# The last expert and the tail of a one-core diffusion step: half of the earlier experts' sum added by an identity product, the last chunk turned at unit 2, the last three units by column halves

## The reference

```
for e in range(8):                       # N_EXPERTS
    g, u = split(h @ w_gu_e[e])          # 1024 -> 2 x 2816
    out += gates[:, e] * ((silu(g) * u) @ w_down_e[e])
x = x + g2 * out                         # g2: a row per condition
y = x * rsqrt(mean(x * x) + 1e-6) * final_norm_g
```

## Time and profile before

| | us |
|---|---|
| time, median of 3 runs (lowest, highest) | 1475.29 (1468.94, 1476.71) |
| time of the profiled execution | 1475.58 |
| its span, first to last instruction | 1473.7 |
| PE busy in the span | 1402.7 (95%) |
| DVE busy | 1123.2 (76%) |
| ACT busy | 817.0 (55%) |
| mean granted TensorE clock | 0.970 |

### The profile page before, as it was taken

One profiled execution on the slowest core, in us unless ns is written; L12 is line 12 of the kernel. 1 busy time (PEld: TensorE's weight loads), 2 busy tenths in 40 slices (PEclk: granted clock), 3 DMA queues, 4 the chain that ended last, 5 costly groups with the idle time before them and its releaser, 6 DMA issues.

```text
span 1473.7 us, 17234 instructions
## 1 busy us (share of the span) xinstructions
PE 1402.7 (95%) x6831; PEld 1157.8 (79%) x6831; DVE 1123.2 (76%) x1026; ACT 817.0 (55%) x811; POOL 227.5 (15%) x333
## 2 busy tenths in 40 slices
PE   5899989999999999989999999999999999999994
PEld 1687557799999986777888888988889888898873
DVE  0798665547777555556899899988989989889994
ACT  2532663523223223355677777776777777777761
POOL 3000480000000023010899100000000000000000
PEclk8999999999999999979999999999999999999996
DMA  9857343945454536527799999999999999999971
GB/s 343 305 200 255 124 143 122 314 149 161 154 176 152 188 139 202 188 91 284 252 389 389 357 412 348 379 379 352 409 363 360 389 334 412 368 360 389 368 275 44
DMA packets 115255, 406.06 MB, mean 276 GB/s; under 512 B 7937, under 2 KB 30642, under 8 KB 97762
## 3 DMA queue, kind: packets, MB, share of 16 engines
q1 hardware_dynamic: 108176, 382.24, 69.8%
q0 software_dynamic: 5920, 19.44, 4.4%
q10 hardware_dynamic: 1074, 3.23, 0.6%
HBM read 394.92 MB, written 9.96 MB: 275 GB/s over the span
## 4 chain that ended last, share of the span: by engine, by line
PE 90%; DVE 5%; DMA 2%; ACT 1%; issue 1%; POOL 0%; DVEq 0%; SPq 0%; POOLq 0%; ACTq 0%
PE ps L1633 26%; PE ps L1635 26%; PE ps L1634 26%; DMA raw<-in_ada_w 2%; PE ps L1978 1%; PE ps L1647 1%; DVE ring_lo L1448 1%; PE ps L1767 1%; PE ps L1788 1%; PE ps L1687 1%; PE ps L1889 1%; PE ps L1708 1%; PE ps L1832 1%; DMA xg<-rows_dram,pick_to 1%; PE ps L1934 0%
## 5 line engine op out<-in xcount | busy, mean ns | idle before, releaser
L1448 DVE TENSOR_TENSOR ring_lo<-raw,ring_hi 128x2048 fp32r<-128x2048 f32 (+1 forms) x210 | 452.1, 2168 | 59.8 <-ACT ring_hi L949 58.0
L949 ACT ACTIVATE ring_hi<-raw 128x2048 fp32r<-128x2048 f32 (+1 forms) x210 | 381.9, 1821 | 139.7 <-PE ps L1635 138.4
L1633 PE MATMUL ps<-ring_hi,xe 128*128 128x512 f32 (+1 forms) x576 | 219.3, 381 | 2.3 <-issue 1.6
L1635 PE MATMUL ps<-ring_lo,xe 128*128 128x512 f32 (+1 forms) x576 | 217.0, 377 | 0.0
L1634 PE MATMUL ps<-ring_hi,xe 128*128 128x512 f32 (+1 forms) x576 | 216.8, 376 | 0.0
L1089 DVE TENSOR_TENSOR ring_lo<-raw,ring_hi 128x2048 fp32r<-128x2048 f32 x53 | 120.4, 2288 | 104.1 <-ACT ring_hi L756 103.9
L756 ACT ACTIVATE ring_hi<-raw 128x2048 fp32r<-128x2048 f32 x53 | 101.1, 1913 | 173.4 <-PE ps L1635 157.4
L1448 DVE TENSOR_TENSOR ring_lo_more<-raw,ring_hi_more 128x2048 fp32r<-128x2048 f32 (+1 forms) x70 | 151.8, 2168 | 20.2 <-ACT ring_hi_more L949 19.9
L949 ACT ACTIVATE ring_hi_more<-raw 128x2048 fp32r<-128x2048 f32 (+1 forms) x70 | 127.4, 1820 | 42.2 <-PE ps L1635 42.2
L1633 PEld LDWEIGHTS ps<-ring_hi,xe 128*128 128x128 f32 x576 | 108.9, 189 | 19.9 <-issue 1.8
L1635 PEld LDWEIGHTS ps<-ring_lo,xe 128*128 128x128 f32 x576 | 108.5, 188 | 17.9
(11 more groups left out here) (299 smaller groups left out, 2424.4 us busy)
## 6 DMA issues: line engine op xcount, KB each, us to landing
raw<-in_w_gu_e SPq DMA_DIRECT2D x128, 1024.0 KB, 7.7
raw<-in_w_down_e SPq DMA_DIRECT2D x88, 1024.0 KB, 8.8
raw<-in_ada_w SPq DMA_DIRECT2D x48, 1024.0 KB, 5.4
raw<-in_w_gu_e SPq DMA_DIRECT2D x64, 768.0 KB, 6.1
raw<-in_w_gu SPq DMA_DIRECT2D x44, 512.0 KB, 4.9
raw<-in_w_qkv SPq DMA_DIRECT2D x12, 1024.0 KB, 11.6
raw<-in_w_down SPq DMA_DIRECT2D x11, 1024.0 KB
raw<-in_w_o SPq DMA_DIRECT2D x4, 1024.0 KB, 6.0
```

What stands on the lines that cost most here:

```text
L949: act.activation(ehi[m % RINGM][:, 0:w], raw[:, (MOE_U0 + m) % RAW, 0:w], ACT.Copy).then_inc(hi_ready, 1)
L1448: dve.tensor_tensor(elo[m % RINGM][:, 0:w], raw[:, (MOE_U0 + m) % RAW, 0:w], ehi[m % RINGM][:, 0:w].bitcast(F32), ALU.subtract).then_inc(l ...
L1633: pe.matmul(out, l_hi, r_hi, start=first, stop=False)
L1635: return pe.matmul(out, l_hi, r_lo, start=False, stop=last)
```

## The change

Five edits. (1) The six folds leave g0 to g5. The left halves of the three tiles (columns 0 to 511) are folded on DVE after the last `lo`. The right halves are not folded: PE adds `acc` into the PSUM bank by a product with the identity matrix, in F32, before the last expert's rows are added to the same bank, and one multiplication by g2 serves both. (2) The last chunk is turned before d2 and split at d2 (TURN_LAST_N), into a buffer of its own (`last_hi`, `last_lo`: the place of `xe` for the other parity of experts). (3) PE does e0, e1, e2 for columns 0 to 511 (bank 4) and then again for columns 512 to 1023 (bank 5), and the left half is brought back between e1 and e2 of the right half. (4) y is scaled by its gate while it is split, slot by slot, in two halves; the six pieces have a PSUM bank each, so that PE does not wait for DVE. (5) The squares are summed by halves, DVE reads `meta` before its first addition, and POOL's pairs of dependent instructions are chained by one shared semaphore (the cut diff leaves that last edit and the lists of semaphores out).

```diff
+TURN_LAST_N = 2
+LAST_UNITS = 3
+        last_ssq = sb("last_ssq", [P, TILES, 2])       # declared after ssq
+        last_hi, last_lo = xe[:, (LAST + 1) % 2, 0], xe[:, (LAST + 1) % 2, 1]
+        COMB_BANKS = ((6, 7, 0), (1, 2, 3))
...
# ScalarE: high_eh
-                if NC * e + c:
+                last = (e, c) == (LAST, NC - 1)
+                if NC * e + c and not last:
                     act.wait_ge(unit_used, used_by("down", *((e, c - 1) if c else (e - 1, NC - 1))))
-                    act.activation(eh_hi[:, 4 * half:4 * half + n, :],
+                    act.activation((last_hi if last else eh_hi)[:, 4 * half:4 * half + n, :],
# keep_y, for the last expert
-                    act.activation(y_hi[:].rearrange("p (a n) -> p a n", a=2), ps[:, 4:6, :],
-                                   ACT.Copy).then_inc(ey_hi_ready, 1)
+                    for half in range(2):
+                        act.wait_ge(y_half, half + 1)
+                        act.activation(y_hi[:, half * HALF:(half + 1) * HALF], ps[:, 4 + half, :], ACT.Copy,
+                                       scale=slot_gate[:, e:e + 1]).then_inc(ey_hi_ready, 1)
# in the loop over units (the same on VectorE with low_eh)
-                if kind == "down" and n == 0 and (e, c) == (LAST, NC - 1):
-                    high_eh(e, c)
+                if kind == "down" and n == TURN_LAST_N and (e, c) == (LAST, NC - 2):
+                    high_eh(e, NC - 1)
...
# VectorE, in the loop over units
-                if kind == "gu" and (e, c) == (LAST, NC - 1) and n < 6:
-                    if n == 0:
-                        dve.wait_ge(acc_loaded, 16)
-                        dve.wait_ge(gbc_sb, 16)
-                    fold(n)
# VectorE, after it
+            def low_y(half):
+                cols = slice(half * HALF, (half + 1) * HALF)
+                dve.wait_ge(ey_hi_ready, half + 1)
+                dve.scalar_tensor_tensor(y_lo[:, cols], ps[:, 4 + half, :], slot_gate[:, LAST:LAST + 1],
+                                         y_hi[:, cols].bitcast(F32), ALU.mult, ALU.subtract).then_inc(ey_lo_ready, 1)
+            def add_last(half, k):
+                n, cols = TILES * half + k, slice(half * HALF, (half + 1) * HALF)
+                if half == 0:
+                    dve.wait_ge(x_folded, k + 1)
                 dve.wait_ge(comb_ps, n + 1)
+                dve.tensor_tensor(acc[:, k, cols], ps[:, COMB_BANKS[half][k], :], gbc[:, COND[k], cols],
+                                  ALU.mult).then_inc(x_scaled, 1)
+                dve.wait_ge(x_scaled, n + 1)
+                dve.tensor_tensor(x[:, k, cols], x[:, k, cols], acc[:, k, cols], ALU.add).then_inc(comb_sb, 1)
+            fold(0)
+            fold(1)
+            low_y(0)
+            fold(2)
             dve.wait_ge(meta_ready, 1)
             blocks = dve.value_load(meta[0:1, EXTRA:EXTRA + 1], min_val=0, max_val=EXTRA)
+            add_last(0, 0)
+            add_last(0, 1)
+            low_y(1)
+            add_last(0, 2)
+            for k in range(TILES):
+                add_last(1, k)
...
# TensorE
+            def bring_back(half):
+                if half:
+                    pe.wait_ge(acc_loaded, 16)
+                    for k in range(TILES):
+                        pe.matmul(ps[:, COMB_BANKS[half][k], :], ident[:], acc[:, k, HALF:], start=True, stop=False)
+                pe.wait_ge(ey_lo_ready, half + 1)
+                for k in range(TILES):
+                    for r, part in enumerate((y_hi, y_lo)):
+                        ins = pe.matmul(ps[:, COMB_BANKS[half][k], :], selT[:, k * P:(k + 1) * P],
+                                        part[:, half * HALF:(half + 1) * HALF], start=(r == 0 and half == 0), stop=(r == 1))
+                    ins.then_inc(comb_ps, 1)
-            for m in range(NM):
+            for m in range(NM - LAST_UNITS):
+                    if n == TURN_LAST_N and (e, c) == (LAST, NC - 2):
+                        pe.wait_ge(eh_ready, NC * e + c + 2)
+                        turn_hidden(e, c + 1)
...
+            pe.wait_ge(eh_lo_ready, 2 * NC * N_EXP)
+            for half in range(2):
+                for n in range(LAST_UNITS):
+                    m = NM - LAST_UNITS + n
+                    pe.wait_ge(lo_ready, MOE0 + m + 1)
+                    for r in range(2):
+                        w = slice(r * D + half * HALF, r * D + (half + 1) * HALF)
+                        ins = mm3(ps[:, 4 + half, :], last_hi[:, 2 * n + r, :], last_lo[:, 2 * n + r, :],
+                                  ehi[m % RINGM][:, w], elo[m % RINGM][:, w], False, n == LAST_UNITS - 1 and r == 1)
+                    if half and n == LAST_UNITS - 2:
+                        bring_back(0)
+                ins.then_inc(y_half, 1)
+            bring_back(1)
```

More of the change, by code:

```diff
@@ L1063, in _ @@
             act.end_ifs()
[L1065 to L1068, removed]
+            for half in range(2):
+                cols = slice(half * HALF, (half + 1) * HALF)
+                for k in range(TILES):
+                    act.wait_ge(comb_sb, TILES * half + k + 1)
+                    act.activation(acc[:, k, cols], x[:, k, cols], ACT.Square, scale=D ** -0.5,
+                                   accum_out=last_ssq[:, k, half:half + 1]).then_inc(ssq_ready, 1)
             yp = t["y_prompt"].rearrange("b p n -> (b p) n")
@@ L1505, in low_eh @@
                     dve.wait_ge(eh_hi_ready, 2 * (NC * e + c) + half + 1)
[L1506 to L1509, removed]
+                    blocks = slice(4 * half, 4 * half + n)
+                    to, high = (last_lo, last_hi) if (e, c) == (LAST, NC - 1) else (eh_lo, eh_hi)
+                    dve.tensor_tensor(to[:, blocks, :], ps[:, 6 + half, 0:n * P].rearrange("p (s n) -> p s n", s=n),
+                                      high[:, blocks, :].bitcast(F32), ALU.subtract).then_inc(eh_lo_ready, 1)
             def hidden(e, c):
@@ L1557, in _ @@
                     if m == NM:
[L1558 to L1561, removed]
                         break
@@ L1572, in _ @@
                         low_xe(e + 1, half, 6 + half)
[L1573 to L1579 removed]
+                if kind == "down" and n == TURN_LAST_N and (e, c) == (LAST, NC - 2):
+                    low_eh(e, NC - 1)
             def add_to_x(n, count, added):
@@ L1979, in turn_hidden @@
                     ins.then_inc(ehT_ps, 1)
-            def bring_back(n):
-                k, half = n // 2, n % 2
-                if k:
-                    pe.wait_ge(comb_sb, n - 1)
-                for r, part in enumerate((y_hi, y_lo)):
-                    ins = pe.matmul(ps[:, 6 + half, :], selT[:, k * P:(k + 1) * P],
-                                    part[:, half * HALF:(half + 1) * HALF], start=(r == 0), stop=(r == 1))
-                ins.then_inc(comb_ps, 1)
+            def bring_back(half):
+                if half:
+                    pe.wait_ge(acc_loaded, 16)
+                    for k in range(TILES):
+                        pe.matmul(ps[:, COMB_BANKS[half][k], :], ident[:], acc[:, k, HALF:], start=True, stop=False)
+                pe.wait_ge(ey_lo_ready, half + 1)
+                for k in range(TILES):
+                    for r, part in enumerate((y_hi, y_lo)):
+                        ins = pe.matmul(ps[:, COMB_BANKS[half][k], :], selT[:, k * P:(k + 1) * P],
+                                        part[:, half * HALF:(half + 1) * HALF], start=(r == 0 and half == 0), stop=(r == 1))
+                    ins.then_inc(comb_ps, 1)
             number_slots(0)
@@ L2056, in _ @@
                 ins.then_inc(unit_used, 1)
-            pe.wait_ge(ey_lo_ready, 1)
-            for n in range(6):
-                bring_back(n)
+            pe.wait_ge(eh_lo_ready, 2 * NC * N_EXP)
+            for half in range(2):
+                for n in range(LAST_UNITS):
[9 more added lines that the diff above has]
+            bring_back(1)
             pe.wait_ge(meta_ready, 1)
```

43 lines of the change are left out of this document (21 added, 22 removed).

## The result

| | before | after |
|---|---|---|
| time, median of 4 runs (lowest, highest), us | 1474.97 (1468.94, 1476.71) | 1438.37 (1437.13, 1439.47) |
| ratio, 95% interval | | 0.9768 [0.9749, 0.9786] |
| span of the profiled execution, us | 1473.7 | 1437.6 |
| PE busy, us | 1402.7 | 1373.4 |
| mean granted clock | 0.970 | 0.980 |

What follows compares the result with a forecast made beforehand. PE was taken to bound the program, but DVE's chain from 1419 to 1440 us. Gains of 8.0 + 2.6 + 3.1 + 0.9 = 14.6 us off the profiled 1475.58, and 0.3 for the median, gave 1461; range 1455 to 1469.

Steps and rivals of the forecast that it cites:

- e0: Down unit near the end of the last expert, where PE meets DVE: start forecast at 1432.6 instead of 1440.56.
- e2: Last expert's down unit whose low part now follows the split: forecast to end at 1434.7, needed at 1435.4.
- The rest: Ahead of 1400 us: POOL's chained semaphore, the extra tile and the gate on slots were to change nothing.
- if the first 1400 us differ: Sign against the forecast: any difference in the program ahead of the last 70 us; no size given.
- Folds and turn: Last expert up to e0: folds removed and last chunk split earlier, so e0 starts at 1432.6, 8.0 us gained.
- Column halves: PE's e0 to e2 by column halves: 36 products without a gap at full clock, 2.6 us gained.
- Tail: From end of y to last addition: PE's identity products beside DVE's folds and additions, 3.1 us gained.
- Branch: Last addition to first scaling: `meta` read moved earlier, 0.6 to 0.7 us stays of 1.59, 0.9 gained.
- One: Rival at e0: a late link makes PE stop there again with a slow unit behind it, 1467.4 us; chance 0.11.
- two: Rival in the last expert: folds did not hold PE up, so their 5.7 us is lost, 1466.7 us; chance 0.09.
- Three, the lost clock: Rival in the last expert's down units and after: PE at 1.2 GHz throughout, 23.1 us added, 1484 us; chance 0.03.

Runs made afterwards that it cites:

- before_moved32: Kernel before with an unused 32-byte tile declared after `ssq`, no instruction changed: 1452.29 us, ratio 0.9865.
- after_six_folds: Changed kernel with the six folds put back on VectorE among the units and no identity products, tiles unmoved: 1443.21 us, ratio 0.9802 against before.
- edits_unmoved: Changed kernel with all five edits, but `last_ssq` placed in the free tile `junk` so no other tile moves: 1458.47 us, ratio 0.9904 against before.
- pe_alone_512: Separate kernel of 512-column fp32r products on TensorE alone, 6 x 6 operand starts, rows 2176 and 8320 bytes apart: 228.9 to 237.8 ns per product.
- pe_grid: Separate kernel, TensorE alone, 512-column products, operand starts in steps of 32 bytes, rows and blocks multiples of 512 apart: 226.7 to 234.3 ns per product.

## Why the prediction was wrong

It failed in one step, the one it gave a sentence to: **"The rest. The chained semaphore on POOL, the extra tile and the gate on slots change neither the number nor the width of what runs ahead of 1400 us: nothing."** Number and width did not change; the time of each product did. The extra tile alone is 21.5 us (before_moved32). Between the traces of before and after the 21.68 us are 10.0 up to the first product of the experts (669.44 to 659.44; some 3.6 of it stood there at the first scores already, where executions scatter by 5) and 11.7 in the expert stage. By the paces the former is some 1100 products by 5.7 ns, 6, and the latter about 2500 by 5.3 (three slots of four 6.3, the fourth 2.5), 13. So the change does not touch the last 70 us alone, as the section on the time before has it, but also the 512-column products of the stages ahead of them. The prediction did name "if the first 1400 us differ" as what would prove it wrong.

The other steps, with 21.68 added to the trace of after:

- *Folds and turn, 8.0.* Forecast d0's low part 1416.5, e0 1432.6; measured 1416.50, 1432.64, with 0.26 of idle (DVE's path ends last here; at its new pace PE is there a little sooner). Put back, the folds cost 5.71 (forecast 5.7 for them). Right.
- *Column halves, 2.6.* The right half was to end at 1442.5; the identity products, which follow it, start at 1420.79 + 21.68 = 1442.47. The clock stayed at 1.00. Right, with some luck: by the new pace the 36 products take some 0.2 us less than by the old one, and the first product behind the stop takes 0.27 more (0.50 to the next).
- *Tail, 3.1.* Identity products 2.6 forecast, 2.58 measured; the last addition's end forecast at 1449.6, measured 1427.94 + 21.68 = 1449.62. Right; that PE's and DVE's paths there end together, as forecast, is why after_six_folds gained nothing on PE.
- *Branch, 0.9.* 0.71 us from the last addition to the scaling, 0.6 to 0.7 forecast. Right. The Trainium skill (Runtime: NRT & Kernel Launch, Instruction fetch mechanics) says that a taken branch to a target outside the fetched window has to wait for the fetch, so the stall there could have changed; with 0.71 in all it stayed about as it was.
- *Rivals.* One and two did not come. Three, the lost clock, did not either: the Trainium skill's rule on short idle times (TensorE: Matmul & The Clock Gate, A second HAM failure mode: psum-queue depth-cycling) does not show in this stretch, not even with the five stops of after_six_folds.

The edits by themselves came to 1458.47, with the forecast of 1461.0 inside their runs (1454.43 to 1462.79). There the terms can be read at the old pace: in edits_unmoved ACT's high part of d0 starts at 1411.11, the first product of e0 at 1429.20 without a stop of PE, the first scaling at 1447.06. With the 3.44 from 1411.11 to 1414.55 added that is 1432.64 and 1450.50, so 14.4 of the 14.6 came.

## What to carry to other kernels

A diff that adds a tile moves every tile declared behind it; look where the operands of the hot instruction lie before calling it free, and compare two versions with the tiles at the same places, or a pad passes for an optimisation. If one instruction form runs at two paces in one trace, here by the slot it reads, ask what the slots differ in: that was 1.5% of this kernel, free. For streams of 512-column fp32r products, let the moving and the stationary tile start alike modulo 256 bytes, with rows and blocks that are multiples of 256 too; other layouts gave other paces in pe_alone_512, and starts off the steps of 32 were not sorted out.

## What the hardware showed that I had not expected

- 512-column fp32r products: 227 ns from one to the next with alike starts modulo 256, 229 with the stationary one 192 bytes further, 232 to 234 at the other steps of 32, with nothing else at work on the core (pe_grid). What in the chip does it, no run shows.
- In before, where only the fourth slot was alike, its units came near 227 ns only in their second half (231.6 over the first six products, 227.6 over the last six).
- One stop of 3.8 us was followed by a clock of 0.50; five of 0.5 to 1.3 us within 19 us left it at 1.00.
- POOL's last pair before the scaling of the third tile got slow. In its timeline after:

```profile
1427.56 0.54 POOL L745 TENSOR_SCALAR msq<-last_ssq 128x1 f32<-128x1 f32 x1
...
1428.84 1.26 POOL L745 TENSOR_SCALAR msq<-last_ssq 128x1 f32<-128x1 f32 x1
1430.18 1.37 POOL L747 TENSOR_TENSOR rstd<-msq,mhalf 128x1 f32<-128x1 f32 x1
```

  and before, for a tile's pair:

```profile
1464.55 0.19 POOL L631 TENSOR_SCALAR msq<-ssq 128x1 f32<-128x1 f32 x1 [1.97 <-ACT acc L1067]
1464.83 0.55 POOL L634 TENSOR_TENSOR rstd<-msq,mhalf 128x1 f32<-128x1 f32 x1
```

  The third scaling waited 0.46 us for it. The first instruction also reads a second operand from a tile now, but the first two pairs after do so too and took 0.54 to 0.65 and 0.56 to 0.58, so that alone is not it. The long pair starts beside DVE's scalings (1428.65 to 1431.14); before, the last pair started ahead of them (1464.88). That they are the cause was not tried.
